# Router logits as 32-column products on four column groups, with filler products before the mask

## The chip, the cores and the metric

The kernel runs on one core of a Trainium2 chip, as one launch. The metric is the device time of that launch in microseconds (us). The engines of the core are named as in the profile: PE is TensorE (its weight loads are listed apart as PEld), DVE is VectorE, ACT is ScalarE, POOL is GpSimd, SP is SyncE, which here only issues transfers. PSUM has eight banks of 512 float32 columns by 128 partitions; the program calls them `PS[:, bank, column]`.

## What is computed

Two residual layers over 256 tokens of width 2048, float32: layer 0 mixes tokens with a bidirectional mLSTM, layer 1 with multi-head latent attention, and each is followed by a mixture of 16 experts with top-2 routing. The part that matters here is the router:

```python
def moe_ffn(xn, router_w, router_b, w_gate, w_up, w_down):
    scores = jax.nn.sigmoid((xt @ router_w).astype(jnp.float32))        # (256, 16)
    sel = scores + router_b.astype(jnp.float32)
    grp_score = jnp.sum(lax.top_k(sel.reshape(-1, N_GROUPS, EXPERTS_PER_GROUP), 2)[0], axis=-1)
    gmask = jax.nn.one_hot(jnp.argmax(grp_score, axis=-1), N_GROUPS, dtype=jnp.bool_)
    masked = jnp.where(jnp.repeat(gmask, EXPERTS_PER_GROUP, axis=-1), sel, -jnp.inf)
    _, eidx = lax.top_k(masked, TOP_K)
    ...
    hg = jnp.einsum('td,edf->tef', xt, w_gate)
    hu = jnp.einsum('td,edf->tef', xt, w_up)
    a = jax.nn.silu(hg) * hu * gates[..., None].astype(xt.dtype)
    y = jnp.einsum('tef,efd->td', a, w_down)
```

`xt` is the normalized input; `router_w` is 2048 x 16 and is shared by both layers.

## The kernel before

Each layer has a projection stage and an expert stage. Every engine has its own program, written out in the order in which it runs, and the engines are held together by counting semaphores (`sem(name)`). There is no scheduler: the order of the source is the order of the queues.

**Projections.** Weights arrive in units of 512 input rows by 512 columns (1 MB) in a ring of 8 slots. `SP` issues a unit once PE has used the one that held the slot (`unit_used`). ACT rounds a unit to a high part (`high`, L1149), DVE subtracts it to get the low part (`low`, L1510), and PE multiplies in `token_unit` (L627): high weights with high tokens, high weights with low tokens, low weights with high tokens, for both blocks of 128 tokens. The last 16 units of a layer's projection stage are those of the output matrix. PE's order there is written out by hand in the code below: between these units stand `turn(b)`, which transposes the block b of 512 columns of the residual X once DVE has added the output to it, and `logits(b)`.

**Router.** `columns` (DVE, L1756) multiplies the transposes by the norm's gain and writes `XTF[l]`, 16 chunks c of 128 model columns by 256 tokens. `logits(b)` (PE, L657) multiplies for each of the two token blocks t the chunks 4b to 4b+3: stationary are the 128 x 128 tokens, moving are the 16 columns of `RW[:, c, :]`, and the sum over all chunks builds up in bank 6 + t. So block b is eight float32 products. Blocks 0 to 2 stand between output units, block 3 behind the last one, in both layers. DVE's `rooted` (L1759) sums the squares, ACT takes the root (L1289) and loads the table of the sigmoid (L1294). ACT's `experts` turns the logits of both banks into scores (L1317), with the root as scale, and then writes the normalized tokens XN in eight pieces (L1322). DVE's `route` (L1766) makes the mask MK in eleven small steps (L1771 to L1795). PE's `route` (L834) turns the mask into positions and counts, five products that wait for `mask_ready`. DVE computes the key (L1806) and the selection (L1823).

**Experts.** For each of 8 pairs of experts, `gather` (PE, L868) picks the tokens of the pair into 128 slots, `pair` (L884) multiplies them by the gate and up matrices (L908) with one expert on the column group 0 to 63 of the array and the other on 64 to 127, then by the down matrix (L940), and `scatter` (L880, L881) brings the result back. In the first pair the gather comes in two halves of 32 records, each right ahead of the products that need it. A pair's weights are 12 transfers of 2 MB; `room` in SP's `experts` lets one go when its slot is free: the first pair's from `unit_used` of the last projection units, those beyond the slots only when the pair has used some. One of them also waits for `logits` in layer 0.

Of the kernel before, what the change touches and what calls it, by code (L numbers as in the profile page):

```python
# [18 lines left out]
P = 128  # L19
D = 2048  # L20
SEQ = 256
NT = SEQ // P
DC = D // P
# [14 lines left out]
ROPE = 64  # L38
# [7 lines left out]
N_EXP = 16  # L46
# [21 lines left out]
C_SIN = C_COS + 2 * ROPE  # L68
C_ALL = C_SIN + 2 * ROPE
MASKED = 1e30  # L70
# [107 lines left out]
def trunk(nc, w, out):  # L178
# [8 lines left out]
    with ctx:  # L187
# [141 lines left out]
        MK = at("MK", area_at + 4 * 9104, [P, NT, N_EXP], f32r)  # L329
        XTF = (XT0, m_["XT"])  # L330

        def head_slots(v, g, cols):
# [260 lines left out]
        def _(pe):  # L593
# [49 lines left out]
            def router_side(l, free, before):  # L643

                def turn(b):
                    for t in range(NT):
                        pe.wait_ge(sem(free), before + 2 * b + t + 1)
                        for k in range(4):
                            c = 4 * b + k
                            last = pe.transpose(PS[:, 4 + t, k * P:(k + 1) * P], X[:, t, c * P:(c + 1) * P], IDENT)  # L650
                        last.then_inc(sem("x_turned"), 1)

                def logits(b):
                    for t in range(NT):
                        pe.wait_ge(sem("x_columns"), 8 * l + 2 * b + t + 1)
                        for c in range(4 * b, 4 * b + 4):
                            last = pe.matmul(PS[:, 6 + t, 0:N_EXP], XTF[l][:, c, t * P:(t + 1) * P], RW[:, c, :],  # L657
                                             start=(c == 0), stop=(c == DC - 1))
                    return last

                return turn, logits

# [139 lines left out]

            turn, logits = router_side(0, "aout_free", 0)
            pe.wait_ge(sem("router_loaded"), 32)
# [26 lines left out]
            turn(3)  # L831
            logits(3).then_inc(sem("logits"), 1)

            def route(l):  # L834

                pe.wait_ge(sem("mask_ready"), l + 1)
                pe.matmul(PS[:, 1, 0:N_EXP], TRI_R[:, :], MK[:, 0, :], start=True, stop=True)
# [262 lines left out]

            turn, logits = router_side(1, "bout_free", 0)
            pe.wait_ge(sem("q_read"), HEADS_B)
# [23 lines left out]
            turn(3)  # L1126
            logits(3).then_inc(sem("logits"), 1)
            route(1)
# [4 lines left out]
        def _(act):  # L1133
# [178 lines left out]
            def experts(l, base):  # L1312
# [3 lines left out]
                for t in range(NT):  # L1316
                    act.activation(m_["SC"][:, t, :], PS[:, 6 + t, 0:N_EXP], ACT.Sigmoid, scale=SSQ[:, 6 + t:7 + t])\  # L1317
                        .then_inc(sem("scores"), 1)
# [176 lines left out]
        def _(dve):  # L1495
# [262 lines left out]

            def rooted(n, out):  # L1759
                dve.wait_ge(sem("square_parts"), 8 * (n + 1))  # L1760
                link(red(SSQ[:, 0:2], SSB[:, :, :], AX.X, ALU.add))
                ts(SSQ[:, 2:4], SSQ[:, 0:2], 1.0 / D, EPS, ALU.mult, ALU.add).then_inc(sem("means"), 1)
                dve.wait_ge(sem("roots"), n + 2)
                dve.reciprocal(out, SSQ[:, 4:6]).then_inc(sem("ffn_norm"), 1)
# [169 lines left out]
            columns(0, V_FFN, 3)  # L1934
            rooted(0, SSQ[:, 6:8])
            route(0)
# [163 lines left out]
            columns(1, V_FFN + 16, 3)  # L2100
            rooted(2, SSQ[:, 6:8])
            route(1)
# [8 lines left out]
def constants():  # L2111
# [9 lines left out]
    c[:, C_MASK + P:C_MASK + 2 * P] = np.where(p >= f, 0.0, MASKED)  # L2121
    c[:, C_LT:C_LT + 16] = np.array([[-TINY if i < j else 0.0 for i in range(4)] for j in range(4)]).reshape(-1)
    inv = np.float32(10000.0) ** (-np.arange(HALF, dtype=np.float32) / HALF)
    for t in range(NT):
# [20 lines left out]
```

## Time and profile before

| | us |
|---|---|
| median of 3 runs | 1754.29 |
| lowest, highest | 1751.32, 1754.47 |
| the profiled execution | 1753.88 |
| its span | 1752.1 |
| PE busy in the span | 1689.9 |
| DVE, ACT busy | 756.4, 493.7 |

All rows are from the one profiled execution; their times count from the start of its span, and layer 0's expert stage starts at about 440 us, layer 1's at about 1275 us.

### The profile page before, as it was taken

How to read it: one execution, taken by the hardware profiler on the slowest of the kernel's cores; microseconds unless marked ns; L12 is line 12 of the kernel's file. 1: busy time of each engine (PE TensorE's matmuls, PEld its weight loads, DVE VectorE, ACT ScalarE, POOL GpSimd, SP SyncE). 2: the span in 40 equal slices, each digit the busy share in tenths (PEclk: the TensorE clock that was granted, in tenths of full speed). 3: DMA queues.
4: the chain of work that ended last, by engine and by line, in shares of the span. 5: the costliest groups of instructions: out<-in, count | busy, mean ns of one | idle time of the engine just before them, and what ended most of it. 6: DMA issues, size and time to landing. Idle time of an engine off the chain costs nothing.

```text
span 1752.1 us, 21040 instructions
## 1 busy us (share of the span) xinstructions
PE 1689.9 (96%) x8834; PEld 1095.5 (63%) x8834; DVE 756.4 (43%) x1276; ACT 493.7 (28%) x649; POOL 51.8 (3%) x32
## 2 busy tenths in 40 slices
PE   7999999999899999999999999999989999999998
PEld 7998777788444443443458999988854443444343
DVE  4775577754222222222246777784422222222222
ACT  4435456542200000000034565664330000000000
POOL 2000000000000000000021000010000000000000
PEclk9999999999899999999999999999989999999999
DMA  9655534464999999999994545454589999999996
GB/s 312 204 184 168 188 123 129 136 211 149 380 420 428 427 428 428 427 427 428 427 373 156 161 133 156 145 173 161 195 341 420 428 428 428 426 428 428 426 428 280
DMA packets 102376, 531.70 MB, mean 303 GB/s; under 512 B 11764, under 2 KB 28680, under 8 KB 76936
## 3 DMA queue, kind: packets, MB, share of 16 engines
q1 hardware_dynamic: 101904, 530.16, 77.0%
q8 instruction: 74, 1.21, 0.3%
q10 hardware_dynamic: 344, 0.13, 0.0%
q14 instruction: 22, 0.18, 0.0%
q0 software_dynamic: 32, 0.02, 0.0%
HBM read 528.19 MB, written 2.10 MB: 303 GB/s over the span
## 4 chain that ended last, share of the span: by engine, by line
PE 85%; DMA 10%; DVE 2%; ACT 1%; issue 1%; ACTq 0%; DVEq 0%; SPq 0%
PE PS L627 31%; PE PS L908 19%; PE PS L940 13%; PE PS L868 7%; PE PS L710 5%; DMA DOUBLE<-in_moe_w_up 5%; DMA OVD<-in_moe_w_up 3%; DMA OVD<-in_moe_w_down 2%; PE PS L880 2%; PE PS L881 1%; PE PS L795 1%; PE PS L1043 1%; PE PS L1069 1%; PE PS L657 1%; ACT AREA L1330 1%
## 5 line engine op out<-in xcount | busy, mean ns | idle before, releaser
L908 PE MATMUL PS<-DOUBLE,AREA 128*64 128x512 f32 x1280 | 350.0, 604 | 22.1 <-DMA DOUBLE<-in_moe_w_up 8.2
L1510 DVE TENSOR_TENSOR LO<-ring,HI 128x2048 fp32r<-128x2048 f32 (+1 forms) x124 | 267.2, 2155 | 182.0 <-ACT HI L1149 181.8
L1149 ACT ACTIVATE HI<-ring 128x2048 fp32r<-128x2048 f32 (+1 forms) x124 | 223.7, 1805 | 275.6 <-PE PS L627 228.5
L908 PEld LDWEIGHTS PS<-DOUBLE,AREA 128*64 128x64 f32 x1280 | 107.5, 139 | 236.4 <-issue 228.9
L908 PE MATMUL PS<-OVD,AREA 128*64 128x512 f32 x512 | 229.6, 596 | 0.0
L1837 DVE TENSOR_TENSOR X<-PS,X 128x512 f32<-128x512 f32 x128 | 82.4, 686 | 331.1 <-PE PS L881 331.1
L940 PE MATMUL PS<-DOUBLE,AREA 128*64 128x512 f32 x640 | 168.2, 594 | 2.1 <-DMA OVD<-in_moe_w_down 0.2
L627 PE MATMUL PS<-HI,XTH 128*128 128x512 f32 (+1 forms) x672 | 159.7, 379 | 1.5 <-ACT HI L1149 1.5
L627 PE MATMUL PS<-LO,XTH 128*128 128x512 f32 (+1 forms) x672 | 152.8, 369 | 0.0
L627 PE MATMUL PS<-HI,XTL 128*128 128x512 f32 (+1 forms) x672 | 152.5, 368 | 0.0
L627 PEld LDWEIGHTS PS<-HI,XTL 128*128 128x128 f32 x672 | 122.9, 188 | 16.4
L627 PEld LDWEIGHTS PS<-LO,XTH 128*128 128x128 f32 x672 | 122.8, 188 | 16.5 <-DVE LO L1510 0.3
L627 PEld LDWEIGHTS PS<-HI,XTH 128*128 128x128 f32 x672 | 121.0, 188 | 18.6 <-ACT HI L1149 2.1
L868 PEld LDWEIGHTS PS<-AREA,XN 128*128 128x128 f32 x1024 | 121.3, 199 | 13.9 <-issue 13.0
L1873 DVE SCALAR_TENSOR_TENSOR Y_lo<-PS,AREA,Y_hi 128x512 fp32r<-128x512 f32 x64 | 48.1, 751 | 189.4 <-ACT Y_hi L1338 183.8
L868 PE MATMUL PS<-AREA,XN 128*128 128x128 f32 x1024 | 124.7, 284 | 0.8 <-DVE AREA L1823 0.8
L1328 ACT ACTIVATE AREA<-PS 128x512 f32<-128x512 f32 x16 | 9.6, 597 | 410.7 <-PE PS L908 410.7
L908 PE MATMUL PS<-WIDED,AREA 128*64 128x512 f32 x256 | 115.6, 595 | 5.5 <-DMA OVD<-in_moe_w_up 5.5
L940 PEld LDWEIGHTS PS<-DOUBLE,AREA 128*64 128x64 f32 x640 | 52.9, 137 | 103.6 <-issue 100.1
L940 PE MATMUL PS<-OVD,AREA 128*64 128x512 f32 x256 | 111.7, 594 | 0.0
L1338 ACT ACTIVATE Y_hi<-PS,AREA 128x512 fp32r<-128x512 f32 x64 | 44.0, 688 | 192.5 <-PE PS L940 192.5
L1846 DVE TENSOR_TENSOR AREA<-PS,VFF 128x512 f32<-128x512 f32 x64 | 44.3, 692 | 102.0 <-PE PS L868 102.0
(291 smaller groups left out, 1828.8 us busy)
## 6 DMA issues: line engine op xcount, KB each, us to landing
DOUBLE<-in_moe_w_gate SPq DMA_DIRECT2D x48, 2048.0 KB, 20.4
DOUBLE<-in_moe_w_down SPq DMA_DIRECT2D x40, 2048.0 KB, 21.8
DOUBLE<-in_moe_w_up SPq DMA_DIRECT2D x32, 2048.0 KB, 23.3
ring<-in_a_w_in SPq DMA_DIRECT2D x48, 1024.0 KB, 5.1
OVD<-in_moe_w_gate SPq DMA_DIRECT2D x16, 2048.0 KB, 24.8
WIDED<-in_moe_w_up SPq DMA_DIRECT2D x16, 2048.0 KB, 22.5
OVD<-in_moe_w_up SPq DMA_DIRECT2D x16, 2048.0 KB, 27.1
OVD<-in_moe_w_down SPq DMA_DIRECT2D x14, 2048.0 KB, 27.3
```

The source lines that it names most:

```text
L627: mm = pe.matmul(PS[:, banks[t], 0:n], lhs(k0 + kk, t)[part], weights[:, kk, 0:n], start=first and kk == 0 and p == 0, stop=last and kk == ...
L710: last = pe.matmul(PS[:, 4 * (b % 2) + ch, 0:SEQ], weights[:, kk, ch * P:(ch + 1) * P], tokens[:, k, :], start=k == 0 and p == 0, stop=k = ...
L868: last = pe.matmul(PS[:, bank, k * P:(k + 1) * P], XN[:, t, c * P:(c + 1) * P], m_["SEL"][:, t, :], start=(t == 0), stop=(t == NT - 1))
L880: pe.matmul(PS[:, 2 + t, :], SCT[:, t * P:(t + 1) * P], YH[:, d, :], start=True, stop=False)
L908: last = pe.matmul(PS[64 * e:64 * e + 64, up, :], m_["XG"][:, c, 64 * e:64 * e + 64], slot(units[e])[:, kk, :], start=(c == 0), stop=(c == ...
L940: last = pe.matmul(PS[64 * e:64 * e + 64, 4 + d, :], m_["AT"][:, c, 64 * e:64 * e + 64], slot(units[e])[:, d, :], start=(c == 0), stop=(c ...
L1149: act.activation(HI[s % 2][:, :, 0:n], ring[PLACE[u]][:, :, 0:n], ACT.Copy).then_inc(sem("hi_ready"), 1)
L1338: act.activation(YH[:, d, :], PS[:, 4 + d, :], ACT.Copy, scale=m_["GS"])\
L1510: tt(LO[PLACE[u]][:, :, 0:n], ring[PLACE[u]][:, :, 0:n], HI[s % 2][:, :, 0:n], ALU.subtract)\
L1837: tt(xs, PS[:, 2 + t, :], xs, ALU.add).then_inc(sem(counted), 1)
L1846: tt(m_["XG"][:, 4 * g:4 * g + 4, :], ps4(2 + g % 2), VFF[:, l, 4 * g:4 * g + 4].unsqueeze(2).broadcast_to([P, 4, P]), ALU.mult)\
L1873: stt(YL[:, d, :], PS[:, 4 + d, :], m_["GS"], YH[:, d, :], ALU.mult, ALU.subtract)\
```

## The change

The logits of a block are computed the other way round: stationary are two neighbouring chunks' router columns (32 columns, of which 16 are wanted), moving are the 256 tokens of chunk c. Chunk 4b + g goes to the column group g of the array (partitions 32g to 32g + 31 of bank 6), so the block is four products, and the four groups of bank 6 hold partial sums with the experts on partitions. Behind block 3 DVE copies the 128 x 256 partial sums to SBUF (`PART`, in the middle of `rooted`), and `logit_sums` on PE multiplies them by a constant 0/1 matrix `C_SUM`, which adds the four groups' wanted rows and leaves both token blocks' logits in bank 7, from where ACT reads them. Then `keep_on` issues four products of 128 stationary by 512 moving columns into bank 0, whose result nobody reads, ahead of the wait for the mask.

```diff
-C_ALL = C_SIN + 2 * ROPE
+C_SUM = C_SIN + 2 * ROPE
+C_ALL = C_SUM + 16
...
+        PART = m_["SIG"][:, 0:SEQ]
...
                 def logits(b):
+
+                    pe.wait_ge(sem("x_columns"), 8 * l + 2 * b + NT)
+                    for g in range(4):
+                        c = 4 * b + g
+                        two = RW[:, c:c + 2, :] if g < 3 else RW[:, c - 1:c + 1, :]
+                        mm = pe.matmul(PS[32 * g:32 * g + 32, 6, 0:SEQ], two.rearrange("p c e -> p (c e)"),
+                                       XTF[l][:, c, :], start=(b == 0), stop=(b == 3))
+                        if b == 3:
+                            mm.then_inc(sem("logit_parts"), 1)
+
+                def logit_sums():
+
+                    pe.wait_ge(sem("parts_copied"), l + 1)
                     for t in range(NT):
-                        pe.wait_ge(sem("x_columns"), 8 * l + 2 * b + t + 1)
-                        for c in range(4 * b, 4 * b + 4):
-                            last = pe.matmul(PS[:, 6 + t, 0:N_EXP], XTF[l][:, c, t * P:(t + 1) * P], RW[:, c, :],
-                                             start=(c == 0), stop=(c == DC - 1))
-                    return last
-
-                return turn, logits
+                        last = pe.matmul(PS[:, 7, N_EXP * t:N_EXP * (t + 1)], PART[:, t * P:(t + 1) * P],
+                                         CON[:, C_SUM:C_SUM + N_EXP], start=True, stop=True)
+                    last.then_inc(sem("logits"), 1)
+
+                return turn, logits, logit_sums
...
             turn(3)
-            logits(3).then_inc(sem("logits"), 1)
+            logits(3)
+            logit_sums()
+
+            def keep_on(bank, *columns):
+
+
+                for n in columns:
+                    pe.matmul(PS[:, bank, 0:n], ONES, X[:, 0, 0:n], start=True, stop=True)
 
             def route(l):
 
+                keep_on(0, 512, 512, 512, 512)
                 pe.wait_ge(sem("mask_ready"), l + 1)
...
                 for t in range(NT):
-                    act.activation(m_["SC"][:, t, :], PS[:, 6 + t, 0:N_EXP], ACT.Sigmoid, scale=SSQ[:, 6 + t:7 + t])\
+                    act.activation(m_["SC"][:, t, :], PS[:, 7, N_EXP * t:N_EXP * (t + 1)], ACT.Sigmoid, scale=SSQ[:, 6 + t:7 + t])\
                         .then_inc(sem("scores"), 1)
...
-            def rooted(n, out):
+            def rooted(n, out, routed=None):
                 dve.wait_ge(sem("square_parts"), 8 * (n + 1))
                 link(red(SSQ[:, 0:2], SSB[:, :, :], AX.X, ALU.add))
                 ts(SSQ[:, 2:4], SSQ[:, 0:2], 1.0 / D, EPS, ALU.mult, ALU.add).then_inc(sem("means"), 1)
+                if routed is not None:
+                    dve.wait_ge(sem("logit_parts"), 4 * (routed + 1))
+                    dve.tensor_copy(PART, PS[:, 6, 0:SEQ]).then_inc(sem("parts_copied"), 1)
                 dve.wait_ge(sem("roots"), n + 2)
...
+    at = p % 32 - np.where(p >= 96, N_EXP, 0)
+    c[:, C_SUM:C_SUM + N_EXP] = at == np.arange(N_EXP)[None, :]
```

PE behind the last output unit of layer 0 reads, before (L650 is `turn`, L657 `logits`, L837 to L842 `route`; CON holds the identity, XT_110 is `XTF[0]`):

```order
L650 MATMUL PS<-CON,X 128x128 [waits aout_free]
L650 MATMUL PS<-CON,X 128x128 x3
L657 MATMUL PS<-RW,XT_110 128x16 [waits x_columns]
L657 MATMUL PS<-RW,XT_110 128x16 x3
L657 MATMUL PS<-RW,XT_110 128x16 [waits x_columns]
L657 MATMUL PS<-RW,XT_110 128x16 x3
L837 MATMUL PS<-MK,TRI_R 128x16 [waits mask_ready]
L838 MATMUL PS<-MK,ONE_R 128x16
```

and after (L653 is `turn`, L662 `logits`, L671 `logit_sums`, L853 `keep_on`, L859 on `route`):

```order
L653 MATMUL PS<-CON,X 128x128 [waits aout_free]
L653 MATMUL PS<-CON,X 128x128 x3
L662 MATMUL PS<-XT_110,RW 32x256 [waits x_columns]
L662 MATMUL PS<-XT_110,RW 32x256 x3
L671 MATMUL PS<-CON,AREA 128x16 [waits parts_copied]
L671 MATMUL PS<-CON,AREA 128x16
L853 MATMUL PS<-X,CON 128x512 x4
L859 MATMUL PS<-MK,TRI_R 128x16 [waits mask_ready]
L860 MATMUL PS<-MK,ONE_R 128x16
```

Eight products became four, with one wait for both token blocks in place of one for each; behind them there are a second round over DVE with two products, and four products that wait for nothing. The blocks 0 to 2 change in the same way, without the sums and fillers. On DVE the same place reads, before (L1761, L1762, L1764 are `rooted`):

```order
L1756 TENSOR_TENSOR XT_110<-PS,VEC 128x4x128 [waits x_turned] x2
L1761 TENSOR_REDUCE SSQ<-SSB 128x2 [waits square_parts]
L1762 TENSOR_SCALAR SSQ<-SSQ 128x2 [waits vector_chain]
L1764 RECIPROCAL SSQ<-SSQ 128x2 [waits roots]
L1771 TENSOR_TENSOR AREA<-AREA,RB 128x32 [waits scores,router_loaded]
```

and after (L1779 is `columns`, L1784 on `rooted`, L1797 the first step of `route`):

```order
L1779 TENSOR_TENSOR XT_110<-PS,VEC 128x4x128 [waits x_turned] x2
L1784 TENSOR_REDUCE SSQ<-SSB 128x2 [waits square_parts]
L1785 TENSOR_SCALAR SSQ<-SSQ 128x2 [waits vector_chain]
L1788 COPY AREA<-PS 128x256 [waits logit_parts]
L1790 RECIPROCAL SSQ<-SSQ 128x2 [waits roots]
L1797 TENSOR_TENSOR AREA<-AREA,RB 128x32 [waits scores,router_loaded]
```

One copy, which waits for PE's block 3, stands between the mean and the reciprocal.

## Rows read from the trace of the kernel before

**Rows 1.** The page: GB/s that the transfers moved, in 40 equal slices.
```profile
GB/s 312 204 184 168 188 123 129 136 211 149 380 420 428 427 428 428 427 427 428 427 373 156 161 133 156 145 173 161 195 341 420 428 428 428 426 428 428 426 428 280
```

**Rows 2.** Windows: from:to, length, busy by engine (instructions), clock, DMA share, GB/s.
```profile
458.00:465.00 7.00, 7.00 (x34) 2.30 (x32) 0.00 (x0) 0.00 (x0) 0.00 (x0) 1.00 0.68 239
1294.00:1300.00 6.00, 6.00 (x32) 2.00 (x30) 0.00 (x0) 0.00 (x0) 0.00 (x0) 1.00 0.54 180
470.00:780.00 310.00, 301.76 (x1572) 137.56 (x1573) 77.54 (x134) 20.93 (x32) 0.00 (x0) 1.00 1.01 426
```

**Rows 3.** Timeline of SP's queue, layer 0: start, length, what.
```profile
438.31 0.33 SPq L469 DMA_DIRECT2D DOUBLE<-in_moe_w_up  x1
...
460.95 0.80 SPq L469 DMA_DIRECT2D DOUBLE<-in_moe_w_down  x2
```

**Rows 4.** Chain of waits, both layers: start, length, what.
```profile
447.32 6.59 PE PS L868 x32
...
467.79 3.77 PE PS L868 x32
...
1283.44 6.66 PE PS L868 x32
```

**Rows 5.** Windows by granted clock (columns as in rows 2).
```profile
439.50:442.90 3.40, 2.12 (x19) 1.86 (x16) 1.20 (x5) 2.38 (x8) 0.00 (x0) 1.00 0.76 299
442.90:453.10 10.20, 7.01 (x32) 6.92 (x33) 4.69 (x20) 8.92 (x8) 0.00 (x0) 0.50 1.01 430
698.90:702.30 3.40, 1.97 (x10) 0.51 (x8) 0.00 (x0) 0.60 (x1) 0.00 (x0) 1.00 1.00 424
```

**Rows 6.** Timeline 439.6 to 447.3 us, all engines.
```profile
439.66 1.96 PE L657 MATMUL PS<-RW,XT 128*128 128x16 f32 x16
439.76 0.69 DVE L1756 TENSOR_TENSOR XT<-PS,VEC 128x512 f32<-128x512 f32 x1 [0.15 <-PE PS L650]
...
442.38 0.42 ACT L1317 ACTIVATE AREA<-PS,SSQ 128x16 f32<-128x16 f32 x2
442.69 9.13 ACT L1322 ACTIVATE XN<-X,SSQ 128x512 f32<-128x512 f32 x8
...
445.70 0.38 PE L837 MATMUL PS<-MK,TRI_R 128*128 128x16 f32 x1 [4.08 <-DVE MK L1795]
...
446.84 0.43 DVE L1823 TENSOR_TENSOR AREA<-CON,AREA 128x256 f32<-128x256 f32 x1
```

**Rows 7.** Timeline 423 to 427 us, around logits block 2.
```profile
423.11 1.28 DVE L1756 TENSOR_TENSOR XT<-PS,VEC 128x512 f32<-128x512 f32 x2
...
425.14 1.85 PE L657 MATMUL PS<-RW,XT 128*128 128x16 f32 x16
...
426.85 0.71 PE L627 MATMUL PS<-HI,HTH 128*128 128x512 f32 x2
```

**Rows 8.** Timeline of PE, 860.9 us on: WIDED and OVD hold two experts' weights.
```profile
860.98 0.59 PE L908 MATMUL PS<-WIDED,AREA 128*64 128x512 f32 x1
861.01 0.59 PE L908 MATMUL PS<-OVD,AREA 128*64 128x512 f32 x1
861.41 0.59 PE L908 MATMUL PS<-WIDED,AREA 128*64 128x512 f32 x1
```

**Rows 9.** Timeline 453 to 455 us: last gather record, first records and weight loads of L908.
```profile
453.63 0.28 PE L868 MATMUL PS<-AREA,XN 128*128 128x128 f32 x1
...
453.84 0.20 PEld L908 LDWEIGHTS PS<-DOUBLE,AREA 128*64 128x64 f32 x4
454.32 0.14 PEld L908 LDWEIGHTS PS<-DOUBLE,AREA 128*64 128x64 f32 x2 [0.29 <-issue]
```

**Rows 10.** Timeline of PE, from L908 back to 128-column products.
```profile
1302.95 1.03 PE L908 MATMUL PS<-DOUBLE,AREA 128*64 128x512 f32 x4
1303.91 1.27 PE L868 MATMUL PS<-AREA,XN 128*128 128x128 f32 x9
```

**Rows 11.** Timeline of layer 1, the scores.
```profile
1278.50 0.42 ACT L1317 ACTIVATE AREA<-PS,SSQ 128x16 f32<-128x16 f32 x2
```

More of the change, by code:

```diff
@@ L801, in head_unit @@
                 token_unit(U_AOUT + k, OUT_BANKS[0][b], HTP, UNIT_K * n, n == 0, n == 3, k == 15, chunks("h", n))
-            turn, logits = router_side(0, "aout_free", 0)
+            turn, logits, logit_sums = router_side(0, "aout_free", 0)
             pe.wait_ge(sem("router_loaded"), 32)
@@ L1099, in _ @@
                 kv_unit(i)
-            turn, logits = router_side(1, "bout_free", 0)
+            turn, logits, logit_sums = router_side(1, "bout_free", 0)
             pe.wait_ge(sem("q_read"), HEADS_B)
@@ L1126, in _ @@
             turn(3)
-            logits(3).then_inc(sem("logits"), 1)
+            logits(3)
+            logit_sums()
             route(1)
@@ L1934, in _ @@
             columns(0, V_FFN, 3)
-            rooted(0, SSQ[:, 6:8])
+            rooted(0, SSQ[:, 6:8], 0)
             route(0)
@@ L2100, in _ @@
             columns(1, V_FFN + 16, 3)
-            rooted(2, SSQ[:, 6:8])
+            rooted(2, SSQ[:, 6:8], 1)
             route(1)
```

## The prediction

> **What bounds the kernel now.** I read the slices of the span first. The core's transfers run at about 427 GB/s through the two expert stages (roughly 440 to 890 us and 1275 to 1735 us) and mostly at less than half of that elsewhere [rows 1], while PE is busy nearly all the span. So there are two regimes: in the projection stages the end is set by PE, in the expert stages by the weight transfers. A long window inside an expert stage confirms it, 426 GB/s at full DMA share, with one hole at the start of each stage, 458 to 465 us and 1294 to 1300 us [rows 2]. In bytes the first hole is 7 us x (1 - 239/426) = 3.1 us of lost transfer, the second 6 x (1 - 180/426) = 3.5 us. The queue of SP tells why the hole is there: the last four free slots are filled from the end of the last projection unit on (438.31), about 8.4 MB or 20 us of transfer, and the next transfer, which needs a slot that the first pair of experts has used up, goes out only at 460.95 [rows 3]; layer 1 shows the same pattern. The first product of the pair starts at 453.84, right behind the gather [rows 9], so the refill is tied to the chain router, mask, gather. An expert stage ends with its transfers; it therefore ends earlier by what moves the last projection unit earlier, plus what shortens the chain from there to the refill, until the hole is closed.
>
> The chain of waits of that stretch runs over the last unit on PE; DVE's add, columns and mean; ACT's root and table load; the scores at 442.38; eleven small DVE steps to the mask, for which PE waits until 445.70 [rows 6]; the selection; then the first half of the gather, L868 x32, 6.59 us. The other half, the same 32 records, takes 3.77 us at 467.79, and the first half of layer 1 6.66 [rows 4]. The windows by clock give the reason: TensorE was granted 0.50 (1.2 GHz) from 442.9 to 453.1 [rows 5], after PE had stood idle from 441.62 on; layer 1 is alike. Nothing on PE's logits (L657) of the last block is in this chain: they end at 441.62, and ACT is ready for them at 442.38 [rows 6].
>
> **The change part by part.**
>
> *Three logits blocks between the out units (b = 0, 1, 2).* They lie on PE, in a stretch where PE never idles, so each counts in full. Before: 8 products with 128x128 stationary tokens and 16 moving columns, 16 records, 1.71 us from the block's first record to the next unit's (425.14 to 426.85) [rows 7]. After: 4 products of 32 stationary columns and 256 moving ones, 8 records. No 32-column product is in the trace; the nearest is L908 with 64 columns. There each of the two column groups starts a record of 512 columns every 0.43 us, side by side and independently of the other [rows 8], and the pair starts together from its first record on, four weight loads within 0.2 us and then two [rows 9]. So a 256-column record is 0.215 us, each product has two, and if the four groups run side by side a block streams 0.43 us. If they ran one by one it would be 8 x 0.215 = 1.72 us. I take the first, since the rows show groups running together. Changing between 128 and fewer columns costs something: after the last gather record at 453.63 the first L908 starts 0.21 us later where the step is 0.11, its first pair takes 0.05 more (the next weights come at 454.32 instead of 454.27) [rows 9], and from the start of four L908 records at 1302.95 two pairs should end at 1303.81, but L868 starts at 1303.91 [rows 10] and its first weight load is not hidden, another 0.1. Together 0.35 us. New block: 0.78 us, 0.92 saved, 2.75 us for three blocks, per layer. The new wait for both halves of the columns has no price: DVE had finished columns of block 2 at 424.39 and PE comes at 425.14 [rows 7]; behind it on PE would stand the next out unit.
>
> The Trainium skill, TensorEngine Tiling (Array Packing), Key Properties, says that changing the tiling mode drains the engine; the 0.1 us at either side agrees with it.
>
> *The last block (b = 3).* It waits for the second half of the columns, which DVE ends at 440.45 [rows 6]; before, half of the block ran earlier. New: start 440.50, streaming 0.5, about 0.17 for the end of a record, so parts at 441.2. DVE's copy of 128x256 from PSUM is not in the trace; between 0.43 (128x256 from SBUF, L1823) and 0.69 us (128x512 with PSUM, L1756) [rows 6] I take 0.45, the size being that of the first: 441.65. The two sums are four records, 0.11 apart with 0.28 for the last, 0.6 us: logits at about 442.3. ACT can take them at 442.38 because of its table load [rows 6], so this costs nothing in layer 0 by a margin of 0.1 us. In layer 1 ACT loads two tables in this stretch and takes the scores at 1278.50 [rows 11], which leaves a wider margin, about 0.4 us. DVE's reciprocal moves behind the copy, to 441.8, still ahead of the scores. SP's wait for the logits delays one transfer that has some 15 us of others ahead of it: nothing.
>
> *The fillers.* Four products of 128 stationary, 512 moving columns, two records each of 0.43: 3.44 us at 2.4 GHz, started at 442.3 and ended at 445.7. The mask's first product started at 445.70 [rows 6]. So they fit with nothing to spare and nothing lost, if the clock is at its upper level. What they buy is the level of the gather: 6.59 - 3.77 = 2.82 us, in layer 1 2.89 [rows 4]. ACT's normalized tokens come in eight steps of 1.14 us from 442.69 [rows 6], two for each of the gather's four groups, so the second group's are there at 447.3 and are wanted at 449.2 at the faster pace; the mask's products gain under 0.1.
>
> *Does the clock hold?* PE is left with holes of about 0.35 us (438.7), 0.9 us (439.6 to 440.5) and 0.5 us (441.2 to 441.7) ahead of the fillers. The trace shows both outcomes: 1.97 us of PE work in 3.4 us at 698.90 left the level up, while 2.12 us from 439.50, most of it 16-column products, was followed by the fall [rows 5]. The last block alone might therefore let the clock fall before the fillers, in some executions; then part of the fillers runs at 1.2 GHz, and the products of the mask come up to 3.4 us late. I take 2.5 us per layer instead of 2.85 for this.
>
> **The sum.** Per layer 2.75 + 2.5 = 5.25, both layers 10.5 us. The chain's part stays under the holes of 3.1 and 3.5 us. Against the profiled execution's 1753.88 that is 1743.4; the median of the runs is 0.4 above it, so I say 1743.5. The three runs shown lie 3 us apart; a median is known to about 0.2%, 3.5 us, hence the bound for faster and slower.
>
> **Rivals.**
> 1. *Groups overlap only in pairs (0.17).* If the two records of a product stay together in program order, the second of one group runs with the first of the next: five steps of 0.215 in place of two. For it: nothing in the trace has four groups; against it: pairs start together at the first record [rows 9]. Block 1.42, saved 0.28 x 3 = 0.85; the last block ends 0.65 later, which delays the scores by 0.5 in layer 0 and 0.2 in layer 1. Total 2 x (0.85 + 2.15) = 6.0: 1747.9. The Trainium skill, TensorE: Matmul & The Clock Gate, Part 3 (what overlaps and what doesn't), says that matmuls start and end strictly in program order, and this rule would give that time if the two records of a product are neighbours.
> 2. *The clock falls before the fillers in most executions (0.13).* Then they take up to 6.9 us under a cover of 3.4, the mask's products come 3.4 late, and the faster gather gives back 2.85: net 0.6 lost per layer. 2 x (2.75 - 0.6) = 4.3: 1749.6.
> 3. *The refill doesn't follow (0.07).* The chain is shorter but the transfers bound it elsewhere; only the out units' 5.5 us remain: 1748.4. Against it: the first refill goes out 7.1 us after the first L908 [rows 3, 9], and nothing else stands between.
> 4. *The column groups run one after another, and the clock holds (0.06).* Block 2.07, 1.1 lost in three, scores 1.2 late, gather 2.85 won: gain 1.1 in all, 1752.8; no change.
> 5. *Slower (0.03).* One by one, and the clock falls before the fillers: per layer 1.1 + 1.2 + 0.6 lost, 1759.7. It decides from a block above about 1.7 us, the old price, with the clock down when the fillers start.
>
> **How the numbers follow.** Forecast 0.54 at 1743.5, its own range 1740.5 (clock held in both layers, blocks near 0.5 us: 2 x (3.6 + 2.85) = 12.9) to 1746. The range to 1749.5 takes in rivals 1 and 3 and half of 2. Faster (below 1750.4): the forecast, 1, 3 and most of 2, 0.87. Same: 0.10. Slower: 0.03.
>
> **What would show it.** In the changed profile: L662 blocks of 8 records with about 0.8 us between neighbours; four L662 records starting almost together; granted clock 1.00 from the last unit through the gather; the first gather half near 3.8 us; fillers ending by the mask; the holes in the transfers shrunk to under 1 us; the refill about 20 us after the end of the last unit instead of 22.7. Wrong: L662 records spaced by 0.2 us one by one, a clock of 0.50 under the fillers, or a hole of the old size.

## The result

| kernel | median us | range | runs | against before |
|---|---|---|---|---|
| before | 1752.70 | 1749.58 to 1754.47 | 5 | |
| changed | 1742.63 | 1740.42 to 1745.46 | 5 | ratio 0.9946, 95% interval 0.9935 to 0.9956 |

The change makes the kernel faster by 0.54%, 9.5 us by the ratio. The profiled execution of the changed kernel, the slowest of its five, took 1745.46 us (span 1743.8 us), 8.4 us less than that of before.

The chain of waits of the changed kernel, layer 0 (start, length, what), answers to [rows 4]: the fillers (L853) are now in it, and the first half of the gather takes as long as the second.

```profile
439.43 4.89 PE PS L853 x8
445.37 3.84 PE PS L890 x32
...
463.10 3.77 PE PS L890 x32
```

Its timeline around logits block 2 answers to [rows 7, 9]: a block is eight records, 0.57 us from its first record to the next unit's, instead of 1.71. All eight weight loads lie within 0.16 us.

```profile
422.70 0.40 PE L630 MATMUL PS<-LO,HTH 128*128 128x512 f32 x1
423.02 0.16 PEld L662 LDWEIGHTS PS<-XT,RW 128*32 128x32 f32 x8 [0.37 <-issue]
423.02 0.64 PE L662 MATMUL PS<-XT,RW 128*32 128x256 f32 x8
...
423.59 0.50 PE L630 MATMUL PS<-HI,HTH 128*128 128x512 f32 x1
```

The timeline behind the last unit, all engines, answers to [rows 6] (L662 logits block 3, L1788 DVE's copy, L671 the sums, L853 the fillers, L1340 the scores, L1821 the mask, L859 the mask's first product):

```profile
437.23 0.64 PE L662 MATMUL PS<-XT,RW 128*32 128x256 f32 x8 [0.78 <-DVE XT L1779]
...
438.01 0.42 DVE L1788 COPY AREA<-PS 128x256 f32<-128x256 f32 x1 [0.57 <-PE PS L662]
...
438.50 0.94 PE L671 MATMUL PS<-CON,AREA 128*128 128x16 f32 x4 [0.62 <-DVE AREA L1788]
...
439.27 5.05 PE L853 MATMUL PS<-X,CON 128*128 128x512 f32 x8
439.47 0.44 ACT L1340 ACTIVATE AREA<-PS,SSQ 128x16 f32<-128x16 f32 x2 [0.27 <-PE PS L671]
...
442.56 0.19 DVE L1821 SCALAR_TENSOR_TENSOR MK<-AREA 128x32 fp32r<-128x32 f32 x1
...
443.76 0.57 PE L859 MATMUL PS<-MK,TRI_R 128*128 128x16 f32 x1
```

The mask was there at 442.75; its first product came at 443.76, behind the fillers. The windows (columns as in rows 2) say why: the clock was at 0.50 from 438.7 to 442.0, so the fillers ran at 1.2 GHz for 2.8 of their 4.5 us, but at 1.00 under the gather, where [rows 5] has 0.50. The hole in the transfers is smaller than in [rows 2], but not closed:

```profile
455.00:461.00 6.00, 6.00 (x30) 2.01 (x28) 0.00 (x0) 0.00 (x0) 0.00 (x0) 1.00 0.86 300
1286.00:1292.00 6.00, 6.00 (x30) 2.01 (x28) 0.00 (x0) 0.00 (x0) 0.00 (x0) 1.00 0.86 311
...
436.00:438.60 2.60, 1.19 (x13) 0.47 (x11) 1.76 (x6) 1.60 (x4) 0.00 (x0) 1.00 1.03 302
438.70:442.00 3.30, 3.30 (x8) 1.75 (x8) 1.75 (x8) 3.02 (x6) 0.00 (x0) 0.50 0.98 417
442.10:449.00 6.90, 6.31 (x43) 5.02 (x41) 2.84 (x12) 6.71 (x7) 0.00 (x0) 1.00 1.00 426
```

In bytes 6 x (1 - 300/427) = 1.8 us and 1.6 us are lost, where it was 3.1 and 3.5. SP's queue, with the first transfer that needs a slot of the first pair, against [rows 3]: 21.2 us after the last projection unit's release instead of 22.6.

```profile
435.04 0.33 SPq L472 DMA_DIRECT2D DOUBLE<-in_moe_w_up  x1
...
456.25 0.80 SPq L472 DMA_DIRECT2D DOUBLE<-in_moe_w_down  x2
```

**Where the 8.3 us of span went**, by the start times of the same instructions in both profiles. T is the first of the last block's transposes, right behind the last unit (438.12 and 434.85 in layer 0).

| stretch | before | changed | difference |
|---|---|---|---|
| layer 0: start to transposes of block 0 | 385.51 | 385.31 | -0.20 |
| layer 0: from there to T (three logits blocks) | 52.61 | 49.54 | -3.07 |
| layer 0: T to the last product with streamed expert weights | 464.86 | 464.57 | -0.29 |
| layer 1: from there to the transposes of block 0 | 341.11 | 340.38 | -0.73 |
| layer 1: from there to T (three logits blocks) | 29.83 | 26.72 | -3.11 |
| layer 1: T to the last product with streamed expert weights | 466.92 | 465.98 | -0.94 |
| end | 11.29 | 11.27 | -0.02 |

The two stretches with the blocks repeat to 0.02 us in every profile of this study with the same logits. The two expert stages don't: three profiles of the kernel before give 464.7 to 465.1 and 465.3 to 466.9. So a single profile weighs the clock's part badly; the experiments below go further.

### The profile page after: what moved, and what is told of

It is laid out like the page before. It is cut to its first block, busy times and chain, and to the rows that moved or that the text cites. A ratio compares the mean times of both kernels' runs of the same rounds, so it can differ in the third digit from the quotient of the medians.

```text
span 1743.8 us, 20962 instructions
## 1 busy us (share of the span) xinstructions
PE 1685.2 (97%) x8794; PEld 1081.7 (62%) x8794; DVE 756.8 (43%) x1278; ACT 493.2 (28%) x649; POOL 51.7 (3%) x32
## 4 chain that ended last, share of the span: by engine, by line
PE 82%; DMA 15%; DVE 1%; ACT 1%; issue 0%; ACTq 0%; SPq 0%; DVEq 0%
PE PS L630 31%; PE PS L930 15%; PE PS L962 13%; PE PS L890 7%; DMA DOUBLE<-in_moe_w_up 6%; PE PS L724 5%; DMA OVD<-in_moe_w_up 5%; DMA OVD<-in_moe_w_down 3%; PE PS L902 1%; PE PS L809 1%; PE PS L903 1%; PE PS L1065 1%; PE PS L1091 1%; PE PS L853 1%; PE PS L1070 0%; ACT AREA L1353 0%
## 5 line engine op out<-in xcount | busy, mean ns | idle before, releaser
L890 PEld LDWEIGHTS PS<-AREA,XN 128*128 128x128 f32 x1024 | 115.7, 192 | 14.3 <-issue 13.0
L890 PE MATMUL PS<-AREA,XN 128*128 128x128 f32 x1024 | 119.1, 277 | 1.2 <-DVE AREA L1849 1.2
## 6 DMA issues: line engine op xcount, KB each, us to landing
DOUBLE<-in_moe_w_gate SPq DMA_DIRECT2D x48, 2048.0 KB, 20.4
WIDED<-in_moe_w_up SPq DMA_DIRECT2D x16, 2048.0 KB, 22.8
```

The costliest lines, as they stand in the source:

```text
L890: last = pe.matmul(PS[:, bank, k * P:(k + 1) * P], XN[:, t, c * P:(c + 1) * P], m_["SEL"][:, t, :], start=(t == 0), stop=(t == NT - 1))
```

## The experiments

In the expectations, "refill" is the first transfer that needs a slot used up by the first pair of experts, and times "after the last transposes" count from T. Three kinds of number are given for each run: the ratio to the kernel before on the same chip with its interval (kernels compared together share those runs), the length of the first gather half in both layers, and the refill after T.

| run | median us | ratio (95%) | first gather half | refill after T |
|---|---|---|---|---|
| before (profile ahead of the prediction) | | 1 | 6.6, 6.7 | 22.8, 23.2 |
| before, two further profiles | 1754.36 and 1752.74, one run each | | 6.5, 6.7 and 6.6, 6.5 | 22.8, 23.2 and 22.8, 23.1 |
| changed (its profile) | 1742.63 | 0.9946 (0.9935 to 0.9956) | 3.8, 3.8 | 21.4, 21.4 |
| changed again | 1740.94 | 0.9930 (0.9917 to 0.9944) | 3.8, 3.8 | 21.4, 20.35 |
| column groups, no fillers | 1743.63 | 0.9950 (0.9937 to 0.9963) | 6.1, 6.7 | 22.6, 23.3 |
| the same, further profile | 1741.07, one run | | 6.35, 5.4 | 22.7, 22.0 |
| fillers alone | 1747.71 | 0.9982 (0.9974 to 0.9991) | 3.8, 3.8 | 20.0, 20.4 |
| one column group | 1749.22 | 0.9985 (0.9976 to 0.9994) | 3.8, 3.8 | 21.2, 21.2 |
| products of blocks 0 to 2 twice | 1745.41, one run | | 3.8, 3.8 | 20.1, 21.4 |
| fillers in the holes too | 1740.92 | 0.9934 (0.9921 to 0.9947) | 3.8, 3.8 | 20.1, 20.35 |
| the same, further profile | 1739.17, one run | | 3.8, 3.8 | 20.1, 20.35 |
| filled holes, last fillers twice | 1744.62 | 0.9954 (0.9939 to 0.9969) | 3.8, 3.8 | 23.2, 23.15 |
| filled holes, and fillers at the start | 1738.82 | 0.9926 (0.9912 to 0.9939) | 3.8, 3.8 | 20.1, 20.3 |

### Each part alone

The changed kernel without the fillers:

```diff
-                keep_on(0, 512, 512, 512, 512)
```

> The changed kernel without the four filler products. Theory A (the gain has two parts: PE time of the blocks between the out units, about 3.1 us per layer, and the clock under the gather): blocks of 8 records about 0.6 us long stay, the clock falls and stays at 0.50 through the first gather half, which takes about 6.6 us; gain about 6 us against the kernel before (ratio 0.9966). Rival B (the blocks alone carry the gain, the fillers do nothing since they end 1.0 us after the mask): ratio as the changed kernel's, 0.9946. Rival C (all of it is the clock): ratio 1.000.

The kernel before with them:

```diff
             def route(l):
 
+                keep_on(0, 512, 512, 512, 512)
                 pe.wait_ge(sem("mask_ready"), l + 1)
```

> The kernel before with the four filler products ahead of the wait for the mask and nothing else. Theory A: the first gather half falls from 6.6 to 3.8 us in both layers; the fillers may run partly at the lower clock and end up to 1 to 1.5 us behind the mask; gain 3 to 5.5 us (ratio about 0.9977), and the hole in the transfers shrinks by half. Rival B: no gain, 1.000. Rival C: the whole gain, 0.9946.

The chains of waits, first the groups without fillers, then the fillers alone:

```profile
444.83 6.08 PE PS L889 x32
464.80 3.77 PE PS L889 x32
```

```profile
445.35 3.84 PE PS L875 x32
463.07 3.77 PE PS L875 x32
```

In the second kernel the logits are those of before and PE goes from them to the fillers without a hole; in its profile the clock did not fall at all around the router, and the fillers ended ahead of the mask. Its timeline of PE:

```profile
439.55 3.68 PE L838 MATMUL PS<-X,CON 128*128 128x512 f32 x8
443.78 0.28 PE L844 MATMUL PS<-MK,TRI_R 128*128 128x16 f32 x1 [0.55 <-DVE MK L1802]
```

Ratios 0.9950 and 0.9982: 8.8 and 3.2 us. Theory A holds in kind: the first run excludes its rival C (all of it is the clock), the second its rivals B (no gain) and C (the whole gain), so neither part is nothing. In size the first is more than the 6 us expected, and the second is at the lower end of 3 to 5.5. The first run's interval (6.5 to 11 us) lies above 6, and does not exclude that run's rival B, the changed kernel's whole gain. So what the fillers add to the column groups is not shown by the medians; what they do in the profiles is shown below.

Before and the groups without fillers were profiled again, to see whether the gather of the profiled execution was a dear one.

> The kernel before, profiled once more. Question: the fillers were worth 3 to 3.5 us in the medians (fillers alone against before) but 5.7 us by the two gathers of the profiles compared. Theory J: the clock's fall and rise lie differently in each execution, so the first gather half takes anything from about 4 to 6.6 us, and the profiled execution of before, with 6.5 and 6.6, was a dear one. Then at least one of four such gathers (this run and the next) is under 6 us. Rival K: it is 6.5 us each time, and the transfers absorb part of the gain.

> The kernel before, a third profile, for the same question and with the same expectations.

> The changed kernel without fillers, profiled once more. Theory J: first gather half of one layer at least under 6 us, refill at a time that follows it. Rival K: 6.0 and 6.6 us again.

The two further profiles of before, one after the other:

```profile
447.35 6.51 PE PS L868 x32
```

```profile
447.66 6.58 PE PS L868 x32
```

and 6.67 and 6.54 us in layer 1: six of six at 6.5 to 6.7, so theory J falls for the kernel before. Only the groups without fillers had one cheap gather, in layer 1 of the further profile:

```profile
442.23 6.35 PE PS L889 x32
...
1273.65 5.40 PE PS L889 x32
```

That execution took 1741.07 us, and its refill in layer 1 went out 22.0 us after T instead of 23.3. So without fillers the clock's return is earlier in some executions, by up to 1.3 us of gather in what was seen, and not in others. The other half of rival K, that the transfers absorb part of the gain, is taken up below, at the delay of the chain.

### Is it the operand order, or the groups side by side?

```diff
-                        two = RW[:, c:c + 2, :] if g < 3 else RW[:, c - 1:c + 1, :]
-                        mm = pe.matmul(PS[32 * g:32 * g + 32, 6, 0:SEQ], two.rearrange("p c e -> p (c e)"),
-                                       XTF[l][:, c, :], start=(b == 0), stop=(b == 3))
+                        two = RW[:, c:c + 1, :]
+                        mm = pe.matmul(PS[0:N_EXP, 6, 0:SEQ], two.rearrange("p c e -> p (c e)"),
+                                       XTF[l][:, c, :], start=(c == 0), stop=(c == DC - 1))
```

> The changed kernel with all 16 chunks in one column group: 16 stationary router columns and 256 moving tokens, accumulated one after another in partitions 0 to 15 of bank 6, so that the operands are swapped but nothing runs side by side; the sums take 16 partitions; fillers stay. Theory A (groups side by side are what pays): a block takes 8 x 0.215 us + 0.3 = 2.0 us against 1.7 before and 0.57 in the changed kernel; about 1 us per layer lost in the out units, scores about 1 us later; only the clock's gain remains, ratio 0.9985 to 1.000. Rival D (the swap pays by itself, since 16-column weight loads are short): a block near 1 us or less, ratio 0.9955 or lower.

```profile
390.36 1.90 PE L662 MATMUL PS<-XT,RW 128*16 128x256 f32 x8
392.19 0.98 PE L653 MATMUL PS<-CON,X 128*128 128x128 f32 x7
```

A block takes 1.83 us, eight steps of 0.22, as the one-by-one price of the prediction said (1.72 and the switch); three blocks of layer 0 take 0.73 us more than before (53.34 against 52.61), and the scores come 5.44 us after T instead of 4.26. The expectation had 2.0 us for a block. What is left of the gain is the clock's, ratio 0.9985; the clock did not fall in either router stage of this profile. Theory A: the swap alone is a loss, the gain is in the groups.

### In which order do products start?

Each product of blocks 0 to 2 a second time, right behind the first, into bank 7; nothing else is changed.

```diff
+                        if b < 3:
+                            pe.matmul(PS[32 * g:32 * g + 32, 7, 0:SEQ], two.rearrange("p c e -> p (c e)"),
+                                      XTF[l][:, c, :], start=True, stop=True)
```

> The changed kernel; each product of the logits blocks 0 to 2 is issued a second time right behind the first, into bank 7, where nobody reads it. Theory A (each column group works off its own products, whatever stands between them in the program): the four groups stay side by side, a block streams 4 steps of 0.215 instead of 2, about 1.0 us from its first record to the next unit instead of 0.57. Rival G (products start strictly in the order of the program, so the repeated one holds up the next group): groups overlap only with the neighbour, 5 steps of 0.43, a block near 2.3 us.

Its timeline of PE; L662 are the block's own products, L667 the repeated ones, and in the program they alternate.

```profile
391.89 0.66 PE L662 MATMUL PS<-XT,RW 128*32 128x256 f32 x8
392.35 0.64 PE L667 MATMUL PS<-XT,RW 128*32 128x256 f32 x8
392.92 1.09 PE L653 MATMUL PS<-CON,X 128*128 128x128 f32 x8
```

All eight records of L662 start before any of L667, although the program has the repeated product of group 0 ahead of the first of group 1. The block takes 1.02 us, 0.45 more, which is four steps of 0.22 instead of two. So the groups work off their own products side by side, and rival 1 of the prediction has no ground here. The Trainium skill, TensorE: Matmul & The Clock Gate, Part 3, says that matmuls start and end strictly in program order; across column groups this trace shows the other order of starts. It also gives the price of a step, and so of the switch: of the single block's 0.57 us two steps are 0.44, and 0.13 are left for the switch back. On the way in, the block starts 0.33 us after the unit's last record, where it was 0.23 before, another 0.10.

### Does the clock have to fall?

In the changed kernel PE has two holes between the last transposes and the fillers, 0.78 and 0.62 us by the timeline above. Two filler products go into them:

```diff
             turn(3)
+            keep_on(0, 448)
             logits(3)
+            keep_on(0, 256)
             logit_sums()
```

> The changed kernel with two more filler products in the two holes of PE ahead of the fillers: 448 moving columns between the last transposes and logits block 3, 256 between block 3 and the sums. Theory A (the fall of the clock ahead of the fillers costs the 1.0 us by which the mask's first product is late in each layer): the clock stays at 1.00 through to the gather, the fillers end with the mask, 1 to 1.5 us less per layer than in the changed profile, time about 1740 and less spread than the changed kernel's 5 us. Rival E (the extra products only delay block 3 and the sums): scores 0.3 us later, no gain or a loss of 0.5 us.

> The kernel with fillers in the holes, profiled once more. Theory A: clock 1.00 from the last unit through the gather in both layers again, both gather halves 3.8 us, refill 20.1 and 20.35 us after the last transposes. Rival: in this execution the clock falls ahead of the fillers as it did in the changed kernel.

> The changed kernel unaltered, beside the next ones on the same chip. Theory A: ratio 0.9945 +- 0.001. In its profile the refill goes out between 20.1 us (clock kept) and 21.4 us (clock fallen ahead of the fillers) after the last transposes.

Windows of the kernel with filled holes, both layers, from its first profile, and then those of the changed kernel run again:

```profile
434.00:444.00 10.00, 8.90 (x42) 4.70 (x40) 6.41 (x25) 7.15 (x12) 0.00 (x0) 1.00 0.81 310
1265.00:1275.00 10.00, 8.94 (x42) 4.61 (x40) 6.27 (x24) 8.23 (x12) 0.00 (x0) 1.00 0.83 321
```

```profile
434.00:444.00 10.00, 8.24 (x34) 4.34 (x32) 5.85 (x22) 7.14 (x11) 0.00 (x0) 0.83 0.82 310
1265.00:1275.00 10.00, 7.42 (x37) 3.94 (x35) 6.41 (x25) 8.37 (x13) 0.00 (x0) 1.00 0.83 319
```

With filled holes the clock stayed at 1.00 in four of four router stages and the refill went out at 20.1 and 20.35 us after T each time; the scores were no later (4.30 us after T). The two kernels that were built on this one, below, add four stages without a fall. In the changed kernel it fell in three of four, and in one of the two stages of the kernel with the blocks' products twice, whose PE program is the same from T on: four of six against none of eight. Each fall put the refill at 21.4: 1.1 to 1.3 us, since the fillers then end that much behind the mask. That step of theory A is shown, but not the word "ahead": the fall came 0.6 us before the first filler, at its start, and 0.1 and 0.8 us behind it. The last is layer 1 of the changed kernel:

```profile
1270.64 5.38 PE L853 MATMUL PS<-X,CON 128*128 128x512 f32 x8
```

```profile
1270.60:1271.40 0.80, 0.80 (x4) 0.51 (x4) 0.00 (x0) 0.79 (x4) 0.00 (x0) 1.00 1.01 430
1271.50:1274.90 3.40, 3.40 (x5) 1.33 (x4) 2.83 (x14) 3.40 (x5) 0.00 (x0) 0.50 1.02 439
```

Nor do these holes always bring the clock down: the kernel with one column group has both, 0.79 and 0.51 us, with nothing in them, and kept the clock up in its two stages; its last block is 1.90 us long where the changed kernel's is 0.64.

What the filled holes are worth in the medians is not shown: 0.9934 (0.9921 to 0.9947) against 0.9946 and, on the other chip, 0.9930 for the changed kernel. The spread of the timed runs was 3.5 us with filled holes, and 5.0 and 3.3 us for the changed kernel, so the expected narrower spread didn't show either. The run that repeats the changed kernel missed its expected ratio, 0.9945 give or take 0.001. One reason why profiles and medians differ is on record: the profiled execution of the changed kernel has the lowest mean clock of its five (0.994; the others 0.995 to 0.998) and is the slowest, and the five lie in time as they do in clock. At 0.998 only some 7 us are spent at the lower level (an estimate, 0.002 x 1740 / 0.5), of 24 in the profile, so the other executions, by this, have fewer falls than that profile shows.

### Does a delay of the chain pass through to the end?

The last fillers twice as many, in the kernel with filled holes:

```diff
-                keep_on(0, 512, 512, 512, 512)
+                keep_on(0, *[512] * 8)
```

> The kernel with fillers in the holes (448 and 256 columns), and eight filler products of 512 columns instead of four ahead of the mask. Theory A (the chain to the first refill sets the hole in the transfers one for one): fillers end 3.44 us behind the mask in each layer, refill 3.4 us later (about 23.5 us after the last transposes), the hole grows to about 5 us, time 6.9 us above the kernel with four (1740.9, so about 1748). Rival F (the transfers have slack at the start of the stage, and later parts of it absorb the delay): less than 2 us above.

```profile
437.51 7.11 PE L821 MATMUL PS<-X,CON 128*128 128x512 f32 x16
444.06 0.57 PE L861 MATMUL PS<-MK,TRI_R 128*128 128x16 f32 x1
```

The refill moved by 3.1 and 2.8 us (expected 3.4), and a window over the hole shows it, 256 GB/s here where the kernel with four fillers has 399 over the same 8 us:

```profile
452.00:460.00 8.00, 8.00 (x40) 2.73 (x38) 0.00 (x0) 0.00 (x0) 0.00 (x0) 1.00 0.71 256
```

```profile
452.00:460.00 8.00, 8.00 (x40) 2.63 (x38) 0.00 (x0) 0.00 (x0) 0.00 (x0) 1.00 0.99 399
```

The stage from T to the last expert product became longer by 1.4 and 2.6 us than in the first profile of the kernel with filled holes (465.21 against 463.79, 465.81 against 463.20), by 3.2 and 3.4 us than in the second (462.02 and 462.42). The median rose by 3.7 us, of 5.9 us that the refill would give and 6.9 that were expected. Two things cloud it. The medians come from different chips, though from ratios it is 0.0020, 3.5 us, as well. And in the one profile of this run the kernel had an early start: its transposes of block 0 began at 383.9 us, where they began at 385.4 us in that of the kernel with filled holes. By this run alone the delay passes through, somewhere between half and all of it.

The 14 profiles of this study settle it better. They have 28 expert stages, here by the refill after T:

| refill after T | stages | T to the last expert product, mean | lowest, highest |
|---|---|---|---|
| 20.0 to 20.4 | 10 | 462.8 | 461.9, 463.8 |
| 21.2 to 22.0 | 7 | 464.3 | 463.5, 466.0 |
| 22.6 to 23.3 | 11 | 465.3 | 464.1, 466.9 |

The stages are of different kernels, but their program from the gather on is the same. From the first to the last group the refill is 2.8 us later and the stage 2.5 us longer; a line through all 28 has a slope of 0.9, with a standard error of 0.1. So nearly all of a delay of the refill passes through, rival F is excluded, and rival K's transfers absorb little. Why the median of the run above rose by 3.7 us only stays open.

### The early start

The 14 profiles fall into two kinds: transposes of block 0 at 385.1 to 385.9 us (nine, the three of before among them), or at 383.4 to 383.9 us (five, the groups without fillers once in each kind). In all nine of the former, and in none of the latter, the clock was at 0.50 for 3.4 us around 20 us, when PE had waited for the first weights. Windows of before and of the fillers alone:

```profile
19.00:23.00 4.00, 4.00 (x21) 4.00 (x22) 4.00 (x5) 4.00 (x4) 0.00 (x0) 0.58 1.05 388
```

```profile
19.00:23.00 4.00, 4.00 (x36) 4.00 (x35) 4.00 (x5) 4.00 (x4) 0.00 (x0) 1.00 1.05 387
```

The two profiles of the groups without fillers show what this costs, first the one with the fall:

```profile
19.36 3.68 PE L724 MATMUL PS<-XTH,HI 128*128 128x256 f32 x16 [2.32 <-ACT HI L1171]
22.84 2.11 PE L724 MATMUL PS<-XTL,HI 128*128 128x256 f32 x16
```

```profile
18.45 2.17 PE L724 MATMUL PS<-XTH,HI 128*128 128x256 f32 x16 [2.62 <-ACT HI L1171]
20.46 2.08 PE L724 MATMUL PS<-XTL,HI 128*128 128x256 f32 x16
```

The same 16 records take 3.48 us from start to start instead of 2.01, 1.5 us more; another 0.9 us was there before these products began, so the fall explains most of the 2.4 us between these two, not all.

So three more fillers went there, on top of the filled holes:

```diff
                 last.then_inc(sem("x0_turned"), 1)
 
+            pe.wait_ge(sem("x0_tmp"), 1)
+            for n in (512, 512, 256):
+                pe.matmul(PS[:, 0, 0:n], IDENT, X[:, 0, 0:n], start=True, stop=True)
```

> The kernel with fillers in the holes, and three more filler products (512, 512, 256 columns, identity as stationary) behind the very first transposes, where PE waits 2.4 us for the first weights. Theory H: in four of six profiles so far the clock was at 0.50 from 19 to 22 us, and in the two without that the last transposes of layer 0 came 1.9 us earlier; with these fillers it never falls there, so about 1.3 us less on average than with the holes alone (ratio about 0.9927). Rival I: the fall is followed by nothing on PE's path, or the fillers delay the first products: 0.9934.

```profile
19.00:23.00 4.00, 4.00 (x35) 4.00 (x35) 4.00 (x5) 3.90 (x5) 0.00 (x0) 1.00 1.05 386
```

The profile has the early start (383.36 us), the median is the lowest of the study, 1738.82 us (1738.30 to 1740.95), ratio 0.9926 (0.9912 to 0.9939). Against the kernel with filled holes (0.9934) the intervals overlap, and one profile doesn't tell an early start that was caused from one that would have come anyway; so it is the fastest version seen, and its last step is not shown.

## Why the prediction was right

The forecast was 1743.5 us, measured were 1742.63, inside the range and near its middle. That it came so near is in part luck: the kernel before came out at 1752.70 us here instead of 1754.29, and the gain was 9.5 us by the ratio (12.3 when the changed kernel was run again on another chip), where 10.5 were forecast. Two of the prediction's numbers don't follow from its sums: 1743.4 and 0.4 make 1743.8, and 1753.88 less 12.9 is 1741.0, not 1740.5; neither matters here. Step by step:

- **What bounds the kernel: right.** Each projection stage passed on what PE saved, and the holes in the transfers shrank with the refill. Doubling the last fillers widened the hole again, and over 28 stages the expert stage followed its refill by 0.9 us per us.
- **The three blocks: right in kind, a little low.** Forecast 2.75 us per layer, measured 3.07 and 3.11: a block saves 1.03 instead of 0.92. The step of 0.22 us was the forecast one, so the term that was too high is the 0.35 us for the switch, which measured 0.23. Four groups do run side by side.
- **The last block: right, and its margin as thin as said.** At the upper clock the scores come 4.30 us after T instead of 4.26. Where the clock had fallen already under the sums (L671 0.94 us instead of 0.62) they came 4.62 after T, 0.36 later. The copy took 0.42, forecast 0.45.
- **The fillers and the clock: right in mechanism, oversized.** The gather went to 3.84 us as forecast. But the clock fell shortly before the fillers or under them in three of the four profiled router stages of this kernel, and then the mask's first product was 1.0 to 1.3 us late. The refill gained 1.4 and 1.8 us in the profiled execution, 1.4 and 2.9 in the next, a mean of 1.9 per layer, where the step "I take 2.5 us per layer" stood. The doubt was named with its two rows; it was weighed too lightly.
- **What was left out.** 0.7 us were won in the projections of layer 1, where not one instruction differs. It shows in all kernels with the new logits, with one group too, and in none with the old ones, and builds up evenly over the first 280 us. Its cause was not looked for; those kernels also have the wider constant table, 16 columns more, and nothing here tells the two apart. It and the blocks' 2 x 0.34 us, 1.4 us together, covered the 2 x 0.6 us by which the clock fell short, so the total was nearer than its parts.

Rival 2 of the prediction, the clock falling before the fillers in most executions, came near to what the profiles show; its price was too high. It had all fillers at the lower clock, the mask's products 3.4 us late; in each of the four stages with a fall the clock was back after 3.4 us, and they were 1.0 to 1.3 us late.

What stays open: the parts alone give 8.8 and 3.2 us, 12.0 together, where the whole gives 9.5 and on another chip 12.3; these agree within their intervals, but the clock's part in the medians is known no better than 1.6 to 4.6 us. The gathers of the profiles would say 5.7, and the two expert stages in the profile of the fillers alone are 5.8 us shorter than the means of the three profiles of before. That profile isn't typical of its twelve timed runs: the three with the lowest mean clock (0.995 and 0.996, the others 0.997 to 0.999) are the three slowest, 1750.1 to 1752.3 us, where the profiled one took 1746.4. No trace shows where their clock fell.

## What to carry to other kernels

Products with few output columns are cheap when the small operand is stationary and each chunk of the sum goes to a column group of its own, with one product by a 0/1 matrix at the end; swapping the operands without the groups is a loss. When PE waits a few microseconds ahead of a stage that everything waits for, products that nobody reads can be worth their place there. They should end no later than the wait, at the lower clock too, since what runs over delays the chain; products in the short holes in front of them kept the clock up in all eight stages profiled, at no cost that was seen, though the medians don't show a gain. And ask what refills the stream behind such a stage: here a microsecond of PE's chain was about a microsecond of transfer, since a slot came free that much earlier.

## What was not expected of the hardware

- Column groups start their products out of program order among each other: eight records of L662 ahead of all of L667, while the program alternates them.
- The same instruction starts at 385.85 or at 383.43 us in two profiles of the groups without fillers, and all 14 profiles divide in this way by whether the clock was at 0.50 around 20 us.
- The clock's fall is not tied to a place: with one and the same PE program it came 0.6 us ahead of the fillers (after 1.19 us of PE work between 436.0 and 438.6), at their start, 0.1 or 0.8 us behind it, or, in two of six stages, not at all. With fillers running it was back after 3.4 us each time; without them, in the two kernels that have none, it took 10.2 us in nine stages of ten and 6.8 in one.
